# Seven products of tile pairs in place of eight in two up projections, weight sums on GpSimd

## The reference

```
def rms_norm(x, g):
    y = x * lax.rsqrt(jnp.mean(x * x, axis=-1, keepdims=True) + EPS)
    return y * g
def swiglu(h, w_up, w_down):
    g, u = jnp.split(h @ w_up, 2, axis=-1)
    return (jax.nn.silu(g) * u) @ w_down
for l in range(2):
    if l == 1: k_new, v_new = shared_kv(x, g_kv, w_kv, g_k_b)
    x = x + 0.5 * swiglu(rms_norm(x, g_ffn1[l]), w_ffn1_up[l], w_ffn1_down[l])
    x = x + mixer(rms_norm(x, g_mix[l])) @ w_out[l]
    x = x + 0.5 * swiglu(rms_norm(x, g_ffn2[l]), w_ffn2_up[l], w_ffn2_down[l])
```

## Time and profile before

| what | value |
|---|---|
| median of 3 runs | 2701.96 us |
| the profiled execution, its own time | 2707.99 us |
| its span in the profile | 2706.3 us |
| mean granted TensorE clock | 0.965 of full speed |
| instructions | 44423, of them 18995 matmuls |

### The profile page before, as it was taken

One profiled execution on the slowest core, in us unless ns is written; L12 is line 12 of the kernel. 1 busy time (PEld: TensorE's weight loads), 2 busy tenths in 40 slices (PEclk: granted clock), 3 DMA queues, 4 the chain that ended last, 5 costly groups with the idle time before them and its releaser, 6 DMA issues.

```text
span 2706.3 us, 44423 instructions
## 1 busy us (share of the span) xinstructions
PE 2585.6 (96%) x18995; PEld 2459.4 (91%) x18995; DVE 1182.1 (44%) x1455; ACT 810.8 (30%) x1019; POOL 101.5 (4%) x205
## 2 busy tenths in 40 slices
PE   6999999999988799999999999999998879999998
PEld 6999999999755599999999999999986559999998
DVE  7333335583354334433454343334543734443343
ACT  5222223443122323222233322222334633222222
POOL 1000000000112100000000100000011020000000
PEclk9999999999889789999999999999997989999999
DMA  5222322222212122223222322322232042223222
GB/s 175 82 85 73 91 80 75 62 67 80 60 56 74 61 63 78 74 82 93 72 68 94 115 78 81 87 80 70 89 121 75 26 146 78 78 69 102 78 60 84
DMA packets 334523, 220.74 MB, mean 82 GB/s; under 512 B 11849, under 2 KB 326497, under 8 KB 334420
## 3 DMA queue, kind: packets, MB, share of 16 engines
q1 hardware_dynamic: 325268, 185.83, 23.8%
q0 software_dynamic: 9152, 33.43, 3.8%
HBM read 206.78 MB, written 12.45 MB: 81 GB/s over the span
## 4 chain that ended last, share of the span: by engine, by line
PE 92%; DVE 5%; ACT 1%; issue 1%; DMA 1%; SPq 0%; POOLq 0%; POOL 0%; DVEq 0%; ACTq 0%
PE psum L519 73%; PE psum L545 6%; PE psum L2156 1%; PE psum L1443 1%; PE psum L1502 1%; PE psum L1494 1%; PE psum L1757 1%; PE psum L1483 1%; PE psum L1740 1%; PE psum L2379 1%; PE psum L1474 0%; PE psum L2202 0%; PE psum L1708 0%; PE psum L2185 0%; DMA x_nat<-in_x_sample 0%
## 5 line engine op out<-in xcount | busy, mean ns | idle before, releaser
L519 PE MATMUL psum<-act_hi,whi 128*128 128x288 f32 (+2 forms) x3504 | 756.1, 298 | 12.4 <-DVE act_lo L786 3.8
L519 PE MATMUL psum<-act_hi,wlo 128*128 128x288 f32 (+2 forms) x3504 | 753.8, 297 | 0.0
L519 PE MATMUL psum<-act_lo,whi 128*128 128x288 f32 (+2 forms) x3504 | 753.1, 297 | 0.0
L519 PEld LDWEIGHTS psum<-act_hi,whi 128*128 128x128 f32 (+2 forms) x3504 | 563.7, 188 | 15.3 <-issue 4.9
L519 PEld LDWEIGHTS psum<-act_lo,whi 128*128 128x128 f32 (+2 forms) x3504 | 564.0, 188 | 0.3
L519 PEld LDWEIGHTS psum<-act_hi,wlo 128*128 128x128 f32 (+2 forms) x3504 | 563.4, 187 | 0.4
L498 DVE TENSOR_TENSOR wlo<-raw,whi 128x2048 fp32r<-128x2048 f32 x190 | 435.4, 2292 | 238.7 <-ACT whi L491 238.5
L491 ACT ACTIVATE whi<-raw 128x2048 fp32r<-128x2048 f32 x190 | 362.0, 1905 | 272.6 <-PE psum L519 268.6
L519 PE MATMUL psum<-h_lo,whi 128*128 128x288 f32 x1408 | 301.9, 295 | 0.0
L519 PE MATMUL psum<-h_hi,wlo 128*128 128x288 f32 x1408 | 301.9, 295 | 0.0
L519 PE MATMUL psum<-h_hi,whi 128*128 128x288 f32 x1408 | 301.9, 295 | 0.0
(11 more groups left out here) (410 smaller groups left out, 2143.2 us busy)
## 6 DMA issues: line engine op xcount, KB each, us to landing
raw<-in_w_ffn_up SPq DMA_DIRECT2D x176, 512.0 KB, 5.0
raw<-in_w_ffn_down SPq DMA_DIRECT2D x64, 384.0 KB, 3.9
raw<-in_w_ffn_down SPq DMA_DIRECT2D x64, 320.0 KB, 3.4
raw<-in_w_out SPq DMA_DIRECT2D x16, 512.0 KB, 4.4
raw<-in_w_in_a SPq DMA_DIRECT2D x14, 512.0 KB, 4.7
raw<-in_w_in_a SPq DMA_DIRECT2D x16, 384.0 KB, 4.0
raw<-in_w_kv SPq DMA_DIRECT2D x12, 512.0 KB, 4.1
vpg<-in_cache_v POOLq DMA_DIRECT2D x16, 384.0 KB, 4.0
```

What stands on the lines that cost most here:

```text
L519: last = pe.matmul(psum[0:width, 4 * j + 2 * m + h, 0:HALF], w[:, k, cols], a[:, k, h * HALF:(h + 1) * HALF], start=(k == 0 and step == 0) ...
```

## The change

In blocks 1 and 3 the up projection is computed by the Winograd form of Strassen's scheme, one level deep. Weights of two neighbouring tiles and activations are cut in 2x2: rows of the weights into output tile one or two of the pair, and into features 0 to 511 and 512 to 1023; the activations into the same two halves of features, and into tokens 0 to 287 and 288 to 575. Seven products of quarters (A11, S1, S2, A12, S3, S4, A22) in place of eight give the pair's two tiles after additions. A product of quarters, a unit, is 24 matmuls. The four weight quarters are loaded into the four half buffers of `raw` (`raw_q`); GpSimd forms the sums S1 to S4 in place (`seven_pool`), each only when the quarter that it overwrites has been split. The four sums t1 to t4 of the activations are formed by GpSimd too, once for each block, from gained copies (`xg0`, `xg1`). `whi` and `wlo` are used as four slots of 1024 columns; each unit is split three units ahead (`ahead(v)` splits unit v+3). The additions of the products are VectorE's (`u1`, `c11`, `c22`, `c12`, `c21`), two products are kept in SBUF by ScalarE (`keep`). The hidden features are cut into four parts of 6, 6, 6 and 4 chunks in place of 12 and 10; a down tile has 256 output features in place of 128, in two units of half the part's chunks. The K/V projection and the end wait for the last addition to x.

```
+SEVEN_PARTS = (6, 6, 6, 4)
+    A11, S1, S2, A12, S3, S4, A22 = range(7)
+    QUARTER = (0, 2, 0, 1, 2, 1, 3)
...
+        BY_PRODUCT = ("b11", "t1", "t2", "b21", "t3", "b22", "t4")
+        p_kept = [tmp[x].rearrange("p (s n) -> p s n", s=2) for x in range(2)]
+        FIRST_BANKS = (0, 2, 4, 0, 2, 4, 0, 6, 2, 4, 0)
...
+        def unit_hi(act, W, v, base=None):
+            if kind == "up" and i in W.SUMS:
+                act.wait_ge(S.sums_ready, W.sums(step, W.SUMS[i]))
+            else:
+                act.wait_ge(S.part_loaded[quarter], W.loads_before(quarter) + W.loaded(quarter, v))
...
+                act.wait_ge(S.part_done, W.done(W.before[v] + 1))
+            act.activation(hi_slots[W.slot[v]][:, 0:n], raw_q[quarter][:, 0:n], ACT.Copy).then_inc(S.part_hi, 1)
...
 def out_act(act, base, g, gains, W):    # t is the tile of the output projection
                 n, j = base + t, t % 2
-                split_hi(act, n + 1, 1 - j)
-                if t == 3:
+                if t < 3:
+                    split_hi(act, n + 1, 1 - j)
+                else:
+                    unit_hi(act, W, 0, base)
+                    unit_hi(act, W, 1, base)
                     act.wait_ge(S.tile_done, n + 1)
-                    gained_hi(act, 0, gains)
-                    gained_hi(act, 1, gains)
+                    for k in range(QD):
+                        act.activation(act_hi[:, k, first_half], xg0[:, k, first_half], ACT.Copy).then_inc(S.b_hi, 1)
+                    act.wait_ge(S.t_ready, W.t(1))
+                    factor_hi(act, W, "t1")
                 act.wait_ge(region_free[j], n // 2 + 1)
                 for m in range(2):
+                    x_gained(2 * t + m)
+                if t == 3:
+                    unit_hi(act, W, 2, base)
...
 def out_dve(dve, base, g, W):
+                    unit_lo(dve, W, 0)
+                    unit_lo(dve, W, 1)
+                    first_lo(0)
+                    first_lo(1)
                 dve.wait_ge(S.tile_done, n + 1)
...
+                if t == 3:
+                    first_lo(2)
+                    first_lo(3)
+                    factor_lo(dve, W, "t1")
+                    unit_lo(dve, W, 2)
                 for m in range(2):
                     sum_square(dve, m, g, 2 * t + m)
...
+        def seven_sp(sp, q, W, base):
+                    for quarter in (0, 2, 1, 3):
...
+                            v = W.pair_at[pair - 1]
+                            sp.wait_ge(S.part_lo, W.lo(v + {0: W.A12, 2: W.S3, 1: W.S4, 3: W.A22}[quarter] + 1))
+                            if quarter == 0:
+                                sp.wait_ge(S.sums_ready, W.sums(pair - 1, 4))
+                        load_up(pair, m + quarter // 2, quarter)
...
+        def seven_pool(pool, W):
+            for pair, v in enumerate(W.pair_at):
+                for quarter in (2, 3):
+                    pool.wait_ge(S.part_loaded[quarter], W.loads_before(quarter) + W.loaded(quarter, v + W.A22))
+                total(a21, a21, a22, ALU.add, S.sums_ready)
+                if pair == 0:
+                    pool.wait_ge(S.xg_ready, W.xg(QD))
+                    total(factors_raw["t1"], factors_raw["t1"], factors_raw["b11"], ALU.subtract, S.t_ready)
+                pool.wait_ge(S.part_lo, W.lo(v + W.A11 + 1))
+                pool.wait_ge(S.sums_ready, W.sums(pair, 1))
+                total(a11, a21, a11, ALU.subtract, S.sums_ready)
+                if pair == 0:
+                    pool.wait_ge(S.xg_ready, W.xg(KD))
+                    pool.wait_ge(S.b_lo, W.factor("t1"))
+                    total(factors_raw["t2"], factors_raw["b22"], factors_raw["t1"], ALU.subtract, S.t_ready)
+                pool.wait_ge(S.part_lo, W.lo(v + W.S1 + 1))
+                pool.wait_ge(S.sums_ready, W.sums(pair, 2))
+                total(a21, a22, a11, ALU.subtract, S.sums_ready)
+                if pair == 0:
+                    pool.wait_ge(S.t_ready, W.t(2))
+                    total(factors_raw["t3"], factors_raw["t2"], factors_raw["b11"], ALU.subtract, S.t_ready)
+                pool.wait_ge(S.part_lo, W.lo(v + W.A12 + 1))
+                total(a12, a12, a11, ALU.subtract, S.sums_ready)
+                if pair == 0:
+                    pool.wait_ge(S.b_lo, W.factor("b21"))
+                    total(factors_raw["t4"], factors_raw["b21"], factors_raw["t2"], ALU.subtract, S.t_ready)
...
+            def up_unit(v, ready=None):
+                pe.wait_ge(S.part_lo, W.lo(v + 1))
...
+                for s, k in order:
+                    for step, (w, a) in enumerate(((hi, factors_hi), (hi, factors_lo), (lo, factors_hi))):
+                        last = pe.matmul(psum[:, bank + s, 0:HALF], w[:, k, s, :], a[name][:, k, :],
+                                         start=(k == 0 and step == 0), stop=(k == QD - 1 and step == 2))
...
+        def seven_dve(dve, q, W, g, gains, nth, norm):
+                    if left is not None:
+                        c21(pair - 1)
+                    if pair == 0:
+                        factor_lo(dve, W, "t2")
+                        factor_lo(dve, W, "b21")
+                        ahead(v)
+                        ahead(v + 1)
+                        factor_lo(dve, W, "b22")
+                        u1(pair)
+                        norm_dve(dve, norm)
+                        factor_lo(dve, W, "t3")
+                        ahead(v + 2)
+                        ahead(v + 3)
+                        c11(pair)
+                        factor_lo(dve, W, "t4")
+                        ahead(v + 4)
+                        c22(pair)
+                        ahead(v + 5)
+                        c12(pair)
+                        ahead(v + 6)
+                    else:
+                        ahead(v)
+                        if left is not None:
+                            h_low(left[0], 0, left[1])
+                            mix(left[0], 1)
+                        ahead(v + 1)
+                        if left is not None:
+                            h_low(left[0], 1, left[1])
+                        ahead(v + 2)
+                        u1(pair)
+                        ahead(v + 3)
+                        c11(pair)
+                        ahead(v + 4)
+                        c22(pair)
+                        ahead(v + 5)
+                        c12(pair)
+                        ahead(v + 6)
+                    mix(ups, 0)
...
+                    dve.scalar_tensor_tensor(x, psum[:, at:at + 4, 0:HALF], 0.5, x, ALU.mult, ALU.add).then_inc(S.down_done, 1)
...
 def kv_pe(pe, nth, norm):
+            pe.wait_ge(S.down_done, sevens[0].down(16))
...
 def end_pe(pe):
-                    pe.wait_ge(S.region_free0, N_TILES // 2)
-                    pe.wait_ge(S.region_free1, N_TILES // 2)
+                    pe.wait_ge(S.down_done, sevens[1].down(16))
```

More of the change, by code:

```diff
@@ new lines, in build, with up_bank @@
+        BY_PRODUCT = ("b11", "t1", "t2", "b21", "t3", "b22", "t4")
+        p_kept = [tmp[x].rearrange("p (s n) -> p s n", s=2) for x in range(2)]
+        FIRST_BANKS = (0, 2, 4, 0, 2, 4, 0, 6, 2, 4, 0)
+        def up_bank(W, pair, i):
+            part = next(x for x, pairs in enumerate(W.pairs_of) if pair in pairs)
+            at = 7 * (pair - W.pairs_of[part][0]) + i
+            if part == 0:
+                return FIRST_BANKS[at if at < 7 else 7 + (at - 7) % 4]
+            return 2 * ((at + 2 * (part % 2)) % 4)
@@ new lines, in down_bank, with both, rinv_both, unit_columns @@
+        def down_bank(tile):
+            return 4 * ((tile + 1 + tile // 4) % 2)
+        def both(bank):
+            return psum[:, bank:bank + 2, 0:HALF]
+        def rinv_both(cols):
+            return rinv[:, cols].unsqueeze(1).broadcast_to([P, 2, cols.stop - cols.start])
+        def unit_columns(W, v):
+            kind, step, _ = W.units[v]
+            if kind == "up":
+                return 1024
+            return SEVEN_PARTS[step // 4] // 2 * 256
+        def unit_quarter(W, v):
+            kind, step, i = W.units[v]
+            return W.QUARTER[i] if kind == "up" else 2 * (step % 2) + i
@@ L2580, in _ @@
             stick_sample_dve(dve, c)
[L2581 to L2582 removed]
+            out_dve(dve, BASE_OUTB, 5, sevens[1])
+            seven_dve(dve, 3, sevens[1], None, None, None, 5)
             end_dve(dve)
```

456 lines of the change are left out of this document (413 added, 43 removed).

## The result

| | before | changed |
|---|---|---|
| median of 6 runs | 2701.64 us | 2728.36 us (2722.74 to 2735.20) |
| ratio | | 1.0085, 95% interval 1.0067 to 1.0104 |
| profiled execution | 2707.99 us | 2726.0 us |

The account below looks back on a forecast made before the run. TensorE, busy 96%, bound the kernel; later pairs would become bound by the load, sum and split loop. Blocks -6.4, K/V +1.5, end +0.6, signals +5.6 gave +1.3 us: 2703.3 by the median, range 2640 to 2735.

Parts of the forecast that it names:

- likeliest case: Up stages: the port holds both engines, a GpSimd sum takes 2.0 to 2.45 us; total 2690 to 2720, chance 0.55.
- rival 3: Up-stage loop: same mechanism but 2.6 us a sum, loop 28.7 us, no part gains; total 2730, chance 0.18.
- the forecast's own slope: Pairs bound by the loop: 0.1 us on a GpSimd sum moves the total by some 6.6 us.
- The wait before S2: First pair of the first part: TensorE waits 6.5 us for t2's low split, behind sums and splits holding each other.
- 89.5 + 2: First part: 89.5 us against 82.5 before, plus 2 us for slower matmuls behind the 6.5 us wait.
- two loops' signals: Signals from GpSimd through ScalarE to VectorE: 0.1 us each, 4 in a loop, 14 loops, +5.6 us in all.
- I take 2.2 us: Price of one GpSimd weight sum over 1024 columns, as two streams and a start, between bounds of 1.0 and 3.7.
- load 3.5: Reload of A22's quarter in a pair's loop, 2x256 KB alone: 3.5 us from low split to landing.
- the lead takes 3.9 off the second: Second pair of a part: three units split ahead shorten it by 3.9 us, to 23.2.
- The walk: VectorE's order from one low split of A22 to the next, load and held sums included: 27.1 us a pair.
- The four-chunk down stage, "1.0": Part four's down projection: h's last chunk is needed 4.8 us later but comes after 7.4 to 8.3; 1.0 us lost.
- The K/V border, "+1.5": Shared K/V projection waits for the last x addition, 1152 from PSUM at 1.4 us, hidden before: +1.5 us.

Follow-up runs that it names:

- experiment 2: Changed kernel with each GpSimd weight sum replaced by two MEMSETs of about the same time that read nothing, tiles left unsummed: 2667.68 us.
- experiment 7: Changed kernel with a GpSimd MEMSET of 480 columns ahead of each of the 88 weight sums: 2755.44 us.
- Experiment 3: Changed kernel with separate buffers for the third and fourth quarter of each part's second pair, loaded ahead: 2686.95 us.
- experiment 1: Changed kernel with GpSimd's 88 weight sums cut to 8 of 1024 columns: 2657.78 us.
- 4: Changed kernel with the 88 weight sums moved to VectorE, factor sums left on GpSimd: 2669.93 us; later set 2675.90, ratio to before 0.9895.
- 8: Changed kernel with all 96 sums on VectorE, t1 and t2 made earlier and the first pair's norm work moved behind needed splits: 2658.49 us.
- 9: Changed kernel with all sums on VectorE, reordered first pair, second buffers and moved K/V border: 2652.36 us; set of five 2644.51, ratio to before 0.9785.
- experiment 5: Changed kernel with the eight factor sums cut to 2 of 144 columns, all weight sums kept: 2722.6 us.
- experiment 6: Changed kernel with the K/V projection's first-tile splits behind the next to last x addition, its first product waiting for that alone: 2726.65 us.

## Why the prediction was right or wrong

It said 2703, by the median, with 2690 to 2720 for its likeliest case and 2640 to 2735 in all. What came, 2728, is rival 3 almost to the number (2730, chance 0.18), and inside the full range by 7 us. Sign and size of the centre were wrong; the mechanism was the one walked. The nearness to rival 3 is in part luck: it put 2.6 us on each sum, where a sum alone takes 2.40. With 2.40 the forecast's own slope gives some 2716, and the rest came from steps that rival 3 had as the forecast had them.

**Right.** The two engines hold each other for whole instructions: the selects' 55 ns were read rightly as the remainder of short ones, and with a long sum they become 1.3 to 2.2 us on a low split, a multiplication, a gate. The Trainium skill (SBUF — State Buffer, Who interferes with whom) has the same rule, and its other half, that a GpSimd instruction which only writes does not contend with VectorE's two inputs, is what experiment 2 shows for these instructions: 2.2 us of MEMSETs, and 1.23 and 1.36 us beside them. The matmuls cost nothing for changing weights at each (a pair of 168 in 22.25 us, 0.1324 each; forecast 22.4). The wait before S2 was 6.97 us (6.5; in block 3 7.9), the one before S3 2.6 us (2.3), both behind the instructions named. A third pair is 5.7 to 6.4 us over TensorE's own time (about 5 of idle time forecast), and low splits end its waits as said, though S1's, the longest in the pair shown above, was not named. The first part, from the output projection's last matmul to the last up matmul, took 94.9 us, where 89.5 + 2 and two loops' signals give 92.3. Its waits, from TensorE's timeline (with the pitch of one matmul, 0.13 us, each is what is given above):

```profile
1002.47 0.37 PE L1364 MATMUL psum<-act_hi,whi 128*128 128x288 f32 x1 [1.94 <-DVE act_lo L1251]
1017.29 0.58 PE L1364 MATMUL psum<-bx_hi,whi 128*128 128x288 f32 x1 [6.68 <-DVE bx_lo L1220]
1029.96 0.37 PE L1364 MATMUL psum<-bx_hi,whi 128*128 128x288 f32 x1 [2.33 <-DVE bx_lo L1220]
```

**Wrong: the loop, by four terms.** The forecast for the pairs of a later part was 22.4, 23.2, 27.0 and 0.4 for signals in each loop; 22.25, 25.3 and 28.3 came in block 1, 22.25, 26.1 and 28.4 in block 3.
- "I take 2.2 us" for a sum: alone it takes 2.40 (minimum 2.37), a sum of 1152 takes 2.67. By the slope of experiment 7, 0.2 us is 8 us; by the forecast's own slope it would be 13. The estimate from the Trainium skill (GPSIMD Engine Reference, 3.1) of 2.25 was low too. The text had named 2.3 us as the point from which the total goes past +8 us.
- "load 3.5": 4.86 and 4.61 us in the chain. Two pieces of 256 KB aren't "alone" here. SyncE issues the six pieces of the other three quarters from 1141.79 on, and these two last, at 1145.89 and 1146.71; the view of DMA (1140 to 1185 in 40 slices) has the engines at 250 to 340 GB/s for 7 us:

```profile
DMA  0029999992000000000000000006979899400000
GB/s 15 0 76 307 250 264 339 282 282 64 0 0 0 0 0 0 15 0 0 0 0 0 0 0 0 0 0 177 297 176 281 234 278 310 133 0 0 0 0 0
```

  The page's row for them all has a median of 3.9 us; the path sees the last ones issued. 1.2 us in 14 loops would be 17 us if all of it counted, the largest single term. Experiment 3 takes it (with sum 1) out of the turn and wins 6.3 us a part.
- "the lead takes 3.9 off the second": it took 3.0 (28.3 - 25.3). That each pair has a loop of its own length was right.
- The walk put every step behind the other. Measured, the turn of 28.4 us is shorter than the walk with the two corrections (27.1 + 0.8 + 1.2 + 0.4 = 29.5), since some of a sum's length falls beside work of VectorE that it doesn't hold; VectorE is busy for 82% of a later part (60.4 of 74 us), not near 90%. The same error is in "0.1 us on a GpSimd sum moves the total by some 6.6 us", measured as 3.8.

**Wrong: the start and the tails.** TensorE was to start at 1.1 instead of 1.9 us; its wait behind the output projection was 2.23 and 2.05 us, as long as before (2.22). The slower matmuls were priced for the wait before S2 alone; another stretch at the lower level, 1030.9 to 1034.2, followed the one before S3. The four-chunk down stage, "1.0", has 2.3 us of waits (27.9 against 25.6). In experiments 1 to 4, 8 and 9 it is still 27.1 to 27.2, so 1.5 us of it does not come from the later pairs' loop; the trace names h's low splits as what ends it. The K/V border, "+1.5", cost 4.6: the text counted the addition (1.37) and not what stands ahead of it in VectorE's list, a split of 2.3 us. That split stood there before too, but had ended 1.3 us before the last matmul started (it began at 1434.54, the matmul at 1438.15); now it begins at 1436.77, 0.2 us before it, since ScalarE's high half is late. Nor did it count what stands behind the addition, the high and low halves of the last two chunks, or the lower clock: a stretch of 3.4 us from 1440.4. At the end of the kernel +0.55 came for +0.6.

Summed over what the change touches: from the output projection's last matmul to the last down matmul +8.5 us in block 1 and +9.7 in block 3, K/V +4.6, end +0.6, together 23.4, where the same sum of the prediction is +1.3; the medians differ by 26.7. The 22.1 us of miss are, by stage, each against the same stage before: the first parts 2.1 and 1.1; parts 2 and 3 2.3 and 2.5 in block 1, 3.1 and 3.5 in block 3, less 0.4 for each of the four that was forecast behind them and did not come; parts 4 1.6 and 1.8, their down stages 1.3 each; and K/V 3.1. The 3.3 us between 23.4 and 26.7 are in no stage that the change touches, and no run here settles them.

**What the rivals' evidence was worth.** Rival 3 was given 0.18, since 2.2 us was held for better known than it was: it came from two streams and a start, in a trace with no row of two streams. A tenth of a us on it was worth more than most other terms, and both neighbours that could have been measured first (a sum's price, a load's landing in company) erred to the same side.

## What to carry to other kernels

Before moving work to an idle GpSimd, write the cycle from load to load through all engines and ask which of its steps read SBUF with two operands on VectorE: beside a GpSimd sum each of them here ended its own time after the sum did. The same sum took 1.22 us on VectorE and 2.40 on GpSimd here, so the fuller engine was the cheaper place: with the 88 weight sums on it the kernel was 1.05% faster than before, with all 96, the order, the buffers and the border mended 2.15%, where GpSimd made it 0.85% slower. Price a load by the last piece of all that go out with it (3.5 us forecast, 4.6 to 4.9 here), and read behind and ahead of a moved wait in the engine's own list.

## What the runs showed of the hardware

- A GpSimd MEMSET (0.50 us for 480 columns, 0.96 us for 1024, 1.24 us for 1360) beside two-operand VectorE instructions left them at 1.23 and 1.36 us; a GpSimd sum beside the same ones made them 2.5 and 3.0 us.
- A sum over 8 columns on GpSimd took 203 ns in the median of 88 and up to 1.19 us (experiment 1). In experiment 5 one over 8 elements of a factor took 0.21 us with no VectorE instruction beside it and 1.19 and 1.32 us beside splits on VectorE, and ended 0.06 and 0.07 us after them: the tiny instruction waited for the long one.
- TensorE with new weights at every matmul ran 288 columns each 0.1324 us, not slower than two matmuls on the same weights (0.1333).
- The granted clock was 0.80 in the 9 us behind a wait of 6.97 us and 1.00 in the 11 us behind one of 3.47 us in the same place. Behind the same two waits of 1.9 and 1.1 us at the K/V border a stretch of 3.4 us at 0.50 followed in one kernel (experiment 6) and none in another (9).
